# Moving half of the second layer's late modulation to the end of the first expert ring, with a held expert stream, early projection weights and a 17th slot

## The reference, cut to what matters

```python
for l in range(DEPTH):                              # DEPTH = 2
    sh_a, sc_a, gt_a, sh_f, sc_f, gt_f = adaln_params(c, w_mod[l], b_mod[l])   # silu(c) @ w_mod + b_mod
    ...                                             # the same for the context tokens, from c_ctx
    hl = modulate(xl, g_attn[l], sh_a, sc_a)        # rmsnorm(x) * (1 + scale) + shift
    out_lat, out_ctx = token_mixers(hl, hc, ...)    # projection, four kinds of attention, output projection
    xl = xl + gt_a * out_lat
    hl = modulate(xl, g_ffn[l], sh_f, sc_f)
    xl = xl + gt_f * expert_choice_ffn(hl, w_router[l], w_gate[l], w_up[l], w_down[l])
    if not last:                                    # context tokens: the same, in layer 0 alone
        ...
return rmsnorm(xl, g_final)
```

## Time and profile before

| what | us |
|---|---|
| median of 3 runs | 2239.25 |
| lowest, highest | 2234.61, 2239.42 |
| the profiled execution, whole | 2232.47 |
| its span | 2230.7 |
| PE busy | 2012.9 (90%) |
| DVE, ACT, POOL busy | 785.7, 501.5, 157.1 |
| DMA | 515.66 MB, mean 231 GB/s |

### The profile page before, as it was taken

The page is one execution under the profiler, slowest core; times in us unless marked ns, Lnnn a source line. Parts: engine busy times, 40 slices in busy tenths (PEclk is TensorE's granted clock), DMA queues, the critical chain, the costliest instruction groups (busy, mean ns, idle before and its releaser), DMA issues. The chain is left out here.

```text
span 2230.7 us, 27197 instructions
## 1 busy us (share of the span) xinstructions
PE 2012.9 (90%) x10622; PEld 962.6 (43%) x10622; DVE 785.7 (35%) x2065; ACT 501.5 (22%) x1174; POOL 157.1 (7%) x155
## 2 busy tenths in 40 slices
PE   5999989999989999999999799889998698887875
PEld 3445455555543332333323556456555233332322
DVE  3322266787761100101001632387776302020203
ACT  3111144454430010000100321254444100000001
POOL 1101000000001001020100101100000000000000
PEclk9999988999999999999999899999999899999998
DMA  9841110000089999999998202100005899999995
GB/s 346 310 141 56 38 38 1 1 1 1 1 326 426 425 384 403 401 374 426 365 409 349 74 19 76 42 35 1 1 1 208 349 427 426 427 426 427 427 426 233
DMA packets 90921, 515.66 MB, mean 231 GB/s; under 512 B 10578, under 2 KB 15612, under 8 KB 36524
## 3 DMA queue, kind: packets, MB, share of 16 engines
q1 hardware_dynamic: 84480, 493.29, 54.4%
q0 software_dynamic: 4416, 15.21, 2.3%
q10 hardware_dynamic: 1900, 5.43, 0.6%
HBM read 498.69 MB, written 15.20 MB: 230 GB/s over the span
## 5 line engine op out<-in xcount | busy, mean ns | idle before, releaser
L662 PE MATMUL psS<-arena 128*64 128x512 f32 (+9 forms) x4544 | 1167.0, 558 | 68.3 <-DMA arena<-in_w_up 28.1
L662 PEld LDWEIGHTS psS<-arena 128*64 128x64 f32 (+4 forms) x4544 | 461.5, 159 | 669.3 <-issue 607.3
L665 PE MATMUL psT<-ident,arena 128*128 128x128 f32 (+2 forms) x936 | 153.3, 292 | 74.8 <-DVE arena L1823 25.5
L1973 DVE TENSOR_TENSOR arena<-arena,psS 128x512 f32<-128x512 f32 x32 | 20.6, 684 | 553.6 <-PE psS L662 553.6
L1164 ACT ACTIVATE arena<-psS 128x128 f32<-128x128 f32 (+5 forms) x150 | 57.2, 411 | 568.8 <-PE psS L662 521.7
L665 PEld LDWEIGHTS psT<-ident,arena 128*128 128x128 f32 (+2 forms) x936 | 110.3, 147 | 161.6 <-issue 104.1
L1164 ACT ACTIVATE arena<-psS,nb 128x768 f32<-128x768 f32 (+2 forms) x200 | 158.9, 794 | 78.7 <-DVE nb L1814 77.2
L662 PE MATMUL psT<-arena 128*32 128x512 f32 x1536 | 174.7, 595 | 0.0
L1809 DVE TENSOR_REDUCE mx<-psS 128x1 f32<-128x768 f32 (+2 forms) x200 | 165.0, 825 | 22.6 <-PE psS L662 21.0
L1164 ACT ACTIVATE arena<-psT 128x512 f32<-128x512 f32 (+4 forms) x211 | 108.5, 516 | 223.8 <-PE psT L665 211.9
L662 PE MATMUL psO<-arena 128*64 128x128 f32 (+2 forms) x1600 | 151.1, 297 | 0.0
(11 more groups left out here) (227 smaller groups left out, 1377.0 us busy)
## 6 DMA issues: line engine op xcount, KB each, us to landing
arena<-in_w_gate SPq DMA_DIRECT2D x116, 1024.0 KB, 20.7
arena<-in_w_up SPq DMA_DIRECT2D x116, 1024.0 KB, 18.5
arena<-in_w_down SPq DMA_DIRECT2D x116, 1024.0 KB, 24.9
arena<-in_w_mod SPq DMA_DIRECT2D x40, 1024.0 KB, 8.0
arena<-in_w_in SPq DMA_DIRECT2D x6, 2048.0 KB, 7.8
gtb<-in_w_mod SPq DMA_DIRECT2D x8, 1024.0 KB, 7.0
arena<-in_w_out SPq DMA_DIRECT2D x8, 512.0 KB, 7.6
arena<-in_w_out SPq DMA_DIRECT2D x2, 2048.0 KB, 14.3
```

Source lines behind the costliest of these rows:

```text
L662: return nc.tensor.matmul(o, lhsT, rhs, start=start, stop=stop)
L665: return nc.tensor.transpose(o, in_, ident[0:n, 0:n])
L1973: last = V.tensor_tensor(ar[:, a:a + 512], ar[:, a:a + 512], bank(2 * g + h), ALU.mult)
```

## The change

1. **Half of the late modulation moves.** Group 4 stays in front of the experts (8 pieces, j = 0 to 7 of the ring). Group 5 becomes the last eight loads of layer 0's ring. PE multiplies four of its pieces between the context and the latent jobs of `combine`, and four behind them, in bank 3. ACT copies the row at step 2 of layer 1's projection; PE turns it at step 13, DVE makes the columns at step 14.
2. **The expert stream is held.** Six expert pieces may be loaded (`AHEAD_OF_GATHER = 6`); the seventh waits for the third gather (`s_g[2]`).
3. **The last stage of layer 0 runs in the order 2, 0, 1**, and `weighted`, `combined` and the split follow it: the context tokens are combined while the last latent group is still being weighted. `combine` uses seven banks, and waits for each group's low part by itself. The root for layer 1's first pair is begun before the last four additions.
4. **Early projection weights.** Of section B, the up projections and rows 0 to 4 of 8 are loaded as soon as the ring's list ends, rows 5 to 7 once the last group is split. At layer 1's start PE runs the first step of section B before it turns tile 2.
5. **17 slots in layer 1.** The buffer for the gates (`gtb`) moves into the arena, which grows; column 35840 of the arena becomes a slot.

```diff
+AHEAD_OF_GATHER = 6
+WIN_EARLY = 5
-MOD_LATE = (3 * L - MOD_FRONT) * KD
+MOD_LATE, MOD_LAST = KD, KD
+LAST_MOD_AT = {"turn": 13, "columns": 14}
...
+def last_order(l):
+    return (2, 0, 1) if l == 0 else (0, 1)
...
-        NSLOT, TILES_AT = (11, 16), (22784, 26624)
+        NSLOT, TILES_AT = (11, 17), (22784, 26624)
...
                 if l:
                     up_projections()
-                for sec, (_, c0, _, nc_) in enumerate(SECTIONS):
+                    sp.wait_ge(z["done"], groups_done(l - 1, NQ - 1, 7, 2))
+                    section_rows(0, 0, WIN_EARLY)
+                    sp.wait_ge(z["yl"], split_tile(l - 1, NQ - 1, last_order(l - 1)[-1]))
+                    section_rows(0, WIN_EARLY, KD)
+                    sp.wait_ge(Z[l - 1]["ffn_done"], l)
+                for sec in range(len(SECTIONS)):
...
-                for j in range(FIRST[l] + NLOAD):
+                for j in range(FIRST[l] + NLOAD + LAST[l]):
...
-                    if l and j == NSLOT[l] - 1:
+                    if l and j == NSLOT[l] - 2:
                         sp.wait_ge(z["fgev"], 4 * L)
...
+                    if l == 0 and j == FIRST[l] + AHEAD_OF_GATHER:
+                        sp.wait_ge(s_g[2], 16)
...
-                for n in late[:8]:
+                for n in late[:6]:
                     late_mod(n)
                 pe.wait_ge(z["fgev"], 4 * l + 4)
                 for n in range(2):
                     if n and l == 0:
-                        late_mod(late[8])
+                        late_mod(late[6])
...
+                        if l == 0 and n == 2 * TC:
+                            pe.wait_ge(z["y"], hidden_tile(l, q, NX - 1))
+                            for m in last_late[:4]:
+                                late_mod(m)
                         take(b)
                         groups = [2] if t < TC else [0, 1]
+                        if h == 0:
+                            pe.wait_ge(z["yl"], split_tile(l, q, groups[-1]))
...
+                    for m in last_late[4:] if l == 0 else ():
+                        late_mod(m)
...
-                        for g in range(NX):
+                        for g in last_order(l) if (q, st) == (NQ - 1, NSTAGE - 1) else range(NX):
...
                         weighted(q, g)
+                        if q == NQ - 1 and l < L - 1 and g == last_order(l)[-1]:
+                            dve.wait_ge(s_sum, 32)
+                            combined(q, range(2 * TC))
+                        if q in COMBINED[l]:
+                            rest(q, g)
                 if l < L - 1:
-                    dve.wait_ge(s_sum, 32)
-                    combined(NQ - 1)
+                    combined(NQ - 1, range(2 * TC, len(CJ) - 4))
+                    pair_root(Z[l + 1], 0)
+                    combined(NQ - 1, range(len(CJ) - 4, len(CJ)))
```

More of the change, by code:

```diff
@@ L265, in backbone_program @@
         LG = sb("LG", 16)
-        AR = 36864
+        AR = 38912
         arena_at = nc.sbuf_base
@@ L397, in slot_filled @@
             i = j % NSLOT[l]
-            earlier = MOD_FILLS[i] + sum(i < NSLOT[k] and (FIRST[k] + NLOAD - 1 - i) // NSLOT[k] + 1 for k in range(l))
+            earlier = MOD_FILLS[i] + sum(i < NSLOT[k] and (FIRST[k] + NLOAD + LAST[k] - 1 - i) // NSLOT[k] + 1 for k in range(l))
             return s_w[i], 16 * (earlier + j // NSLOT[l] + 1)
         def late_bank(g):
-            return 7 - (g - MOD_FRONT)
+            return 7 if g == MOD_FRONT else 3
         def groups_done(l, q, st, g):
@@ L783, in _ @@
                 for tau in range(NSTEP + 4):
-                    for t in EARLY.get(tau, ()):
+                    for t in EARLY.get(tau, ()) if l == 0 or tau else ():
                         turned(t)
@@ L809, in _ @@
                         last.then_inc(z["proj"], 1)
+                    for t in EARLY.get(tau, ()) if l and tau == 0 else ():
+                        turned(t)
                     b = tau - 1
@@ L844, in _ @@
                             job("Q", 0, r)
+                    if l and tau == 3:
+                        pe.wait_ge(s_mrow, 3 * L)
+                    if l and tau == LAST_MOD_AT["turn"]:
+                        mod_transpose(MOD_FRONT + 1, 5)
                     for i in k_jobs(tau - 1):
@@ L1032, in _ @@
                 gates(5, "fg", (0, 1, 2, 3))
-                late = range(MOD_FRONT * KD, len(MOD_CHUNKS)) if l == 0 else ()
-                for n in late[:8]:
+                late = range(MOD_FRONT * KD, (MOD_FRONT + 1) * KD) if l == 0 else ()
+                for n in late[:6]:
                     late_mod(n)
@@ L1038, in _ @@
                     if n and l == 0:
-                        late_mod(late[8])
+                        late_mod(late[6])
                     pe.wait_ge(z["dup"], 2 * l + n + 1)
                     tr(bank(4 + n, 0, P, 0, 48), ar[0:48, F["DUP"] + n * P:F["DUP"] + n * P + P], 48).then_inc(z["dupT"], 1)
-                for n in late[9:]:
+                for n in late[7:]:
                     late_mod(n)
-                for g in range(MOD_FRONT, 3 * L) if l == 0 else ():
+                for g in (MOD_FRONT,) if l == 0 else ():
                     mod_transpose(g, late_bank(g))
@@ L1120, in group @@
                         experts, n, col = range(QUAD), CAP_C, 256
+                        for e in experts if (q, st) == (NQ - 1, NSTAGE - 1) else ():
+                            pe.wait_ge(*slot_filled(l, (q * NSTAGE + st) * QUAD + e))
                     for h in range(2):
@@ L1450, in _ @@
                         modulated(x, 6 + x % 2)
-                    for g in range(NX if q in COMBINED[l] else 0):
-                        act.wait_ge(z["y"], hidden_tile(l, q, g))
+                    for g in (last_order(l) if q == NQ - 1 else range(NX)) if q in COMBINED[l] else ():
+                        act.wait_ge(z["y"], hidden_tile(l, q, last_group(l, q, g)))
                         for h in range(2):
@@ L1612, in _ @@
                         mod_columns(MOD_T_AT[tau])
+                    if l and tau == LAST_MOD_AT["columns"]:
+                        mod_columns(MOD_FRONT + 1, 5)
                     if tau < NSTEP and uses_dve(*STEPS[tau]):
```

86 lines of the change are left out of this document (50 added, 36 removed).

## The result

| | before | after |
|---|---|---|
| median of 8 runs each, us | 2236.57 (2233.21 to 2240.05) | 2223.04 (2215.22 to 2227.70) |
| profiled execution: its time, span, mean granted clock | 2232.47, 2230.7, 0.967 | 2215.22, 2213.4, 0.970 |

The ratio over all runs is 0.9932 with a 95% interval of 0.9918 to 0.9946. The medians are 13.5 us apart and the means (2236.55 and 2221.54) 15.0, where 13.1 were forecast, and the median is the 2223 us of the forecast.

The account below looks back on a forecast made before the run. PE was taken to bound layer 0's experts and DMA layer 1's. The terms -6.4 - 2.3 - 2.9 - 1.5 sum to -13.1 us, from a mean of 2236.4 to a forecast of 2223, range 2214 to 2234.

Parts of the forecast that it names:

- Part 1: Start of layer 0's experts: with emptied queues the third gather lands 7.0 us earlier, less 0.6 for half-clock turns: -6.4 us.
- loses 1.7 us to the clock: Layer 0's first expert stage: PE loses about 1.7 us to reduced clock both before and after the change.
- Rival A: Layer 0's gathers gain half, as queues take turns: -3.1 instead of -6.4, sum -9.8, 2227 us; chance 0.17.
- Part 2: Layer 0's first quad: PE's waits for expert weights behind the store of X go: -2.3 us.
- A wait for expert weights in the first quad: Layer 0's experts: the prediction called itself wrong if PE waits for expert weights there; no size given.
- 3 us to spare: Layer 0's seventh stage: piece 27 lands at T + 67.8, needed at T + 71.0; T is the third gather's landing.
- Part 3: Joint from layer 0's last expert matmul to layer 1: new order and filled waits give -2.9 us, bounds 0 to -5.
- The turn to the squares: Layer 1's start, first turn to section B's first squares: warm turns and the moved step give -1.9 us.
- The early weights: Section B's weights at layer 1's start: early, and not last before either, so no gain was counted.
- Part 4: Layer 1's 17th slot: 2.46 us of stream loaded sooner, less 1.0 us later start: -1.5 us.
- Rivals B: Gather gains are given back, as POOL's descriptor work sets landing: only -2.3 left, 2234 us; chance 0.10.
- C: Joint becomes the longer way: PE falls to half clock there, +17.3 us; kernel +7, 2243 us; chance 0.05.

Follow-up runs that it names:

- no_hold: The changed kernel without the wait of the seventh expert piece for the third gather: median 2231.36 us, 0.9967 of the kernel before.
- again: The changed kernel as it is, run once more: median 2219.26 us, 0.9911 of the kernel before.
- ahead8: The changed kernel with eight expert pieces instead of six loaded ahead of the hold: median 2218.72 us, 0.9919 of the kernel before.
- ahead4: The changed kernel with four expert pieces instead of six loaded ahead of the hold: median 2224.61 us, 0.9953 of the kernel before.
- pieces0: The changed kernel with all eight last modulation pieces behind the latent jobs, none in the middle: median 2227.18 us, 0.9963 of the kernel before.
- thinlast: The changed kernel with seven of eight late modulation pieces cut to one 32-column matmul: median 2217.36 us, 0.9914 of the kernel before.
- latewin: The changed kernel with section B's weights issued only after layer 0's experts, up projections behind them: median 2221.26 us, 0.9931 of the kernel before.

## Why the prediction was right

**Part 1, -6.4: the mechanism right, the size too small.** From the first gather's issue to the first matmul 17.8 became 9.7; with the issue 0.2 later, the start moved by 7.9. The third gather was taken to land 6.4 us behind its issue, at 679.5; it landed at 678.6, 5.3 us behind: what layer 1's second took before (5.4). The queues drained where forecast (share 0.22, then 0.00). What failed is the sentence that the first stage loses 1.7 us to the clock "in both": with no wait between the turns the clock is back at 1.00 by 678, and the stage takes 7.09. *no_hold* (three waits, granted clock 0.50 up to 696, 8.77 us) ties this to the waits. So the part was worth 7.9 + 1.7 = 9.6 us. The loss of 0.6 for half-clock turns is real (1.06 for 0.74 at the first tile), but the third was turned in 0.75.

Rival A counted the gathers and the loads as sharing the DMA engines byte for byte, which made the part -3.1. The runs decide against that size: 8.4 us between *no_hold* and *again*. The traces show why. What the two queues moved (q1 holds the loads, q0 the gathers: packets, MB, share of 16 engines) in 674.6 to 686.4 us of the kernel before, and then in 670.2 to 679 us of after, where q1 has no row:

```profile
q1 hardware_dynamic: 470, 3.45, 69.1%
q0 software_dynamic: 431, 1.57, 32.5%
```
```profile
q0 software_dynamic: 432, 1.57, 54.3%
```

The two queues move nearly the same number of packets side by side, but a packet of the loads has 7.3 KB and one of the gathers 3.6, so the gathers get a third of the bytes and not half. Their packets take 11.6 us from the first to the last in before and 5.9 in after, and the first starts 4.3 us behind the first issue instead of 1.9. That is 5.7 + 2.4 = 8.1 us, the whole way from 13.4 to 5.3. The rule that rival A named, from the Trainium skill (DMA: Bandwidth & Descriptors, Queues, rings and completion order), says that an engine takes turns between the queue rows with work, one packet at a time. The trace agrees with it; it was the equal bytes that were wrong. *ahead8* shows the queue's weight in small: 2.1 MB more ahead of the gathers, 1.9 us.

**Part 2, -2.3: the step that failed.** Of the two waits, 0.97 + 1.31, one of 1.28 is left; over all of layer 0 they went from 5.4 to 4.6 us, so 0.8 was gained (3.7 to 4.7 in the seven profiles whose layer 0 has the same stream). A wait for expert weights in the first quad was one of the prediction's own signs of being wrong, and it is there. The "3 us to spare" were used from both sides. With T = 678.67 piece 27 was wanted at 747.37 = T + 68.7 and not T + 71.0, since PE began 0.6 us sooner behind T and without its clock loss of 1.7. It was there at 748.65 = T + 70.0 and not T + 67.8. The start of the stream is not at fault: the first held piece landed 5.1 us behind its issue, as forecast. The four pieces that share the engines with the second quad's gathers took 14.5 us to land where 13.5 were counted, and X with two pieces 13.6 where 12.3 were; why is not shown. 3.2 - 2.3 - 2.2 is the wait of 1.3. *ahead4* shows the same cover running out: two pieces less, 3.89 us of wait. Parts 1 and 2 together were forecast at -8.7 and are -10.6 at E (1233.18 to 1222.57).

**Part 3, -2.9: the sum right, its terms less so.** The first turn at E + 17.9 (forecast 17.5), warm as said. The turn to the squares gained 3.3 us more where 1.9 were taken, and some of it went again before the gates. E to the gates is -3.1 in the two profiles, and -2.7 between the means of two kernels with the old joint (210.8, 213.4) and the nine with the new one unedited (207.7 to 211.5, mean 209.4); single profiles scatter by 2 us each way. The pieces do fill PE's wait for the split (*pieces0*); the last four, forecast at 3.5 us on the path, cost with the first four 2.3 (*thinlast*). The early weights, which the forecast put at nothing, carry 4.1 us of the way to the squares (*latewin*). What the new order of the last stage is worth by itself was not tested.

**Part 4, -1.5: the sign right, half the size.** The later start is +1.1 to 1.5 us (forecast 1.0), the shorter stream -1.8 to -1.9 (forecast -2.46); by the means of all profiles the two make -0.8.

**The sum.** Parts 1 to 4 in the two profiles: -10.6, -3.1, -0.7 are -14.4 against -13.1. The profiles' other 2.9 us lie in stretches that the change leaves as they were, below. Part 1 gave 3.2 us more than forecast, part 2 1.5 less and part 4 0.7 less. That the sum comes out within 1.3 us of the forecast is partly luck, and so is the agreement of the median, since the same kernel gained 11.4 us on one chip and 18.9 on another. Rivals B and C are out: the gathers landed early, and the granted clock was 1.00 from E to 1250 us.

## What to carry to other kernels

A small load that somebody waits for is worth clearing the queues for: hold the bulk loads back until it lands, and take away what is already queued ahead of it, since either alone can give nothing. Count what a small transfer loses beside a full queue in packets and not in bytes: here a packet of the loads was twice as large as one of the gathers. How much may be held back is set by the next large transfer that the stream has to absorb: work out both when a piece lands and when it is wanted, with the clock that the consumer will then have. And look for waits on a split, a copy or a root as places for matmuls that are due later; they also keep the next ones at full clock.

## What the runs showed that was not expected

Stretches of unchanged code come in two lengths. From the gate columns to the opening of layer 1's loads it took 246.2 us in after and *ahead8* and 247.7 to 248.5 in the other twelve; from there to the first gather 51.65 or 53.35 us. That the first two profiles fell on different sides is 3.7 of their 17.3 us. The tail, from the start of the last combination to the end, took 20.8 to 21.1 us in five profiles and 21.8 to 22.2 in nine; after is 0.8 us longer there than before, which takes back what its seventeenth slot gave. The start of the kernel up to the late modulation, the same instructions in all, took 653.4 to 662.4 us. Among the eight runs of after the mean granted clock goes with the time: 0.970 at 2215.22 and 2215.56, 0.962 at 2227.70. So a profile gives the place of a gain, and only medians of several runs give its size.
